# Inversion of the chunk matrices: levels 16 and 32 computed as two column halves, level 64 as one quadrant

## The reference, cut to what matters

```python
L = jnp.where(tri_strict, jnp.einsum('bhnid,bhnjd->bhnij', k_beta, kc) * decay, 0.0)
A = L + jnp.eye(C, dtype=f32)
rhs = jnp.concatenate([vc * bc[..., None], k_beta * jnp.exp(gc)[..., None]], axis=-1)
sol = lax.linalg.triangular_solve(A, rhs, left_side=True, lower=True, unit_diagonal=True)
```

## Time and profile before

| | value |
|---|---|
| median of 3 runs | 2764.27 us (2758.3 to 2764.56) |
| profiled execution | 2765.13 us, its span 2763.1 us |
| PE busy | 2565.5 us, 93% of the span |
| DVE, ACT, POOL busy | 1444.8, 1075.4, 918.6 us |
| L1429 MATMUL | x384 records, 53.0 us, mean 284 ns |
| L1447 and L1444 MATMUL | x256, 280 ns and x128, 226 ns |
| inversion, layer 1 | 491.0 to 581.5 us of the span |
| inversion, layer 2 | 1619.9 to about 1713 us |

### The profile page before, as it was taken

One profiled execution on the slowest core, in us unless ns is written; L12 is line 12 of the kernel. 1 busy time (PEld: TensorE's weight loads), 2 busy tenths in 40 slices (PEclk: granted clock), 3 DMA queues, 4 the chain that ended last, 5 costly groups with the idle time before them and its releaser, 6 DMA issues. The chain is left out here.

```text
span 2763.1 us, 32968 instructions
## 1 busy us (share of the span) xinstructions
PE 2565.5 (93%) x12929; PEld 2070.7 (75%) x12929; DVE 1444.8 (52%) x2609; ACT 1075.4 (39%) x1872; POOL 918.6 (33%) x402
## 2 busy tenths in 40 slices
PE   5989899899989999989988989999999997899998
PEld 3767768797867888757676878877788886786787
DVE  5289748654535541136993766454344206726323
ACT  3345464245332232243554523543333223236532
POOL 0532231112434444334222211134344443332343
PEclk8999999999999999999999989999999999999999
DMA  6211325643234432222132465422223324731232
GB/s 236 76 62 62 123 69 145 186 133 135 96 103 137 137 102 91 93 92 76 47 123 68 116 165 179 146 87 92 76 92 107 93 98 125 152 101 47 77 121 77
DMA packets 339836, 299.93 MB, mean 109 GB/s; under 512 B 56974, under 2 KB 319460, under 8 KB 338660
## 3 DMA queue, kind: packets, MB, share of 16 engines
q1 hardware_dynamic: 287716, 279.49, 32.5%
q10 hardware_dynamic: 51968, 18.35, 2.7%
HBM read 267.89 MB, written 29.93 MB: 108 GB/s over the span
## 5 line engine op out<-in xcount | busy, mean ns | idle before, releaser
L273 PE MATMUL ps<-hh,split 128*128 128x512 f32 x3808 | 1291.6, 407 | 39.4 <-POOL split L220 24.5
L220 POOL TENSOR_TENSOR split<-ring,split 128x1024 fp32r<-128x1024 f32 (+2 forms) x342 | 814.6, 2383 | 1428.4 <-ACT split L216 1428.4
L273 PEld LDWEIGHTS ps<-hh,split 128*128 128x128 f32 x3808 | 729.0, 191 | 212.5 <-POOL split L220 39.7
L273 PE MATMUL ps<-hl,split 128*128 128x512 f32 x1904 | 753.2, 396 | 0.0
L216 ACT ACTIVATE split<-ring 128x1024 fp32r<-128x1024 f32 (+2 forms) x342 | 347.6, 1018 | 893.1 <-PE ps L273 686.1
L273 PEld LDWEIGHTS ps<-hl,split 128*128 128x128 f32 x1904 | 365.4, 192 | 73.1 <-issue 8.4
L273 PE MATMUL ps<-split 128*128 128x512 f32 x1152 | 285.4, 405 | 9.0 <-DVE split L1095 7.1
L273 PEld LDWEIGHTS ps<-split 128*128 128x128 f32 x1152 | 218.6, 190 | 70.6 <-issue 14.7
L2169 PE MATMUL ps<-split 128*128 128x512 f32 x1056 | 240.2, 389 | 0.0
L2169 PEld LDWEIGHTS ps<-split 128*128 128x128 f32 x1056 | 198.1, 188 | 41.0
L560 POOL TENSOR_TENSOR split<-ring,split 128x1024 fp32r<-128x1024 f32 x32 | 76.1, 2378 | 338.2 <-ACT split L552 338.2
(11 more groups left out here) (408 smaller groups left out, 3178.2 us busy)
## 6 DMA issues: line engine op xcount, KB each, us to landing
ring<-in_w_in_dram SPq DMA_DIRECT2D x60, 1024.0 KB, 5.3
ring<-in_w_up_dram SPq DMA_DIRECT2D x44, 1024.0 KB, 5.1
ring<-in_w_ada_dram SPq DMA_DIRECT2D x64, 512.0 KB, 3.7
ring<-in_w_in_dram SPq DMA_DIRECT2D x34, 512.0 KB, 5.2
big<-in_w_ada_dram SPq DMA_DIRECT2D x16, 1024.0 KB, 8.5
ring<-in_w_down_dram SPq DMA_DIRECT2D x16, 896.0 KB, 4.6
ring<-in_w_swa_out_dram SPq DMA_DIRECT2D x8, 1024.0 KB, 5.0
ring<-in_w_dn_out_dram SPq DMA_DIRECT2D x8, 1024.0 KB, 5.0
```

The costliest lines, as they stand in the source:

```text
L220: on.tensor_tensor(halves(pt, nk)[1], slot(n, nk)[:, :, e * P:(e + 1) * P], halves(pt, nk)[0], ALU.subtract).then_inc(low_made, 1)
L273: ins = nc.tensor.matmul(ps[bank[gt]][0:m, :], w[:, k, :], r[:, k, :], start=(k == 0 and w is w_high and r is rhs[0]), stop=(k == nk - 1 a ...
```

## The change

It replaces the products of 128 rows by 128 stationary columns by smaller ones.

- Levels 16 and 32, first product: two matmuls for each head, one for each half of 64 columns (`HALVES`). Stationary are 64 columns of `lows`, moving are the 32 even-block columns of that half of `inv`; the results go to partitions 0 to 63 and 64 to 127 of the same 32 PSUM columns.
- Levels 16 and 32, second product: likewise two for each head, with 64 columns of `invt` stationary and 32 columns of `pc` moving.
- The masks of these levels have 32 columns in place of 64 and the DVE operation 128 columns in place of 256. The update of `inv` becomes two DVE operations of 64 partitions and 128 columns.
- Level 64: the first product takes the 64 rows and 64 columns that matter. A copy of 64 partitions replaces the mask. The second product contracts over 64 rows instead of 128. The mask `level64` goes; the table of constants is 128 columns narrower.

```diff
-    for s in LEVELS:
-        col = np.array([c for c in range(P) if (c // s) % 2 == 0])
-        parts[f"level{s}"] = ((np.arange(P)[:, None] // s) == (col[None, :] // s + 1))
+    for s in LEVELS[:-1]:
+        col = np.array([c for c in range(P // 2) if (c // s) % 2 == 0])
+        parts[f"level{s}"] = ((np.arange(P)[:, None] % (P // 2) // s) == (col[None, :] // s + 1))
...
+                    def pc(c, s):
+                        return wk[:, 8 + c % 2, 0:P if s < 64 else 2 * P].rearrange("p (h c) -> p h c", h=4)
+                    def product(e, rows, s):
+                        return ps[3 + e][rows, 0:P if s < 64 else 2 * P].rearrange("p (h c) -> p h c", h=4)
+                    HALVES = (slice(0, 64), slice(64, 128))
...
-                                        ins = nc.tensor.matmul(ps[3 + e][:, 64 * n:64 * n + 64], lows(g, c)[:, n, :],
-                                                               even_blocks(inv(g, c)[:, n, :], s), start=True, stop=True)
+                                        if s == LEVELS[-1]:
+                                            ins = nc.tensor.matmul(product(e, HALVES[1], s)[:, n, :],
+                                                                   lows(g, c)[0:64, n, 64:128], inv(g, c)[0:64, n, 0:64],
+                                                                   start=True, stop=True)
+                                            continue
+                                        for own in HALVES:
+                                            ins = nc.tensor.matmul(product(e, own, s)[:, n, :], lows(g, c)[:, n, own],
+                                                                   even_blocks(inv(g, c)[:, n, own], s), start=True, stop=True)
...
-                                            ins = nc.tensor.matmul(ps[5 + e][0:64, 64 * n:64 * n + 64], pc(c)[:, n, :],
-                                                                   invt(g, c)[:, n, 64:128], start=True, stop=True)
-                                        else:
-                                            ins = nc.tensor.matmul(ps[5 + e][:, 64 * n:64 * n + 64], invt(g, c)[:, n, :],
-                                                                   pc(c)[:, n, :], start=True, stop=True)
+                                            ins = nc.tensor.matmul(ps[5 + e][0:64, 64 * n:64 * n + 64], pc(c, s)[64:128, n, :],
+                                                                   invt(g, c)[64:128, n, 64:128], start=True, stop=True)
+                                            continue
+                                        for own in HALVES:
+                                            ins = nc.tensor.matmul(ps[5 + e][own, 32 * n:32 * n + 32], invt(g, c)[:, n, own],
+                                                                   pc(c, s)[:, n, :], start=True, stop=True)
...
-                                    nc.vector.tensor_tensor(pc(e), ps[3 + e][:, 0:256].rearrange("p (h c) -> p h c", h=4),
-                                                            over_heads(const(f"level{s}")), ALU.mult).then_inc(d_pc, 1)
+                                    if s == LEVELS[-1]:
+                                        nc.vector.tensor_copy(pc(e, s)[64:128], product(e, HALVES[1], s)).then_inc(d_pc, 1)
+                                    else:
+                                        nc.vector.tensor_tensor(pc(e, s), product(e, slice(0, P), s),
+                                                                over_heads(const(f"level{s}")), ALU.mult).then_inc(d_pc, 1)
...
-                                        ev = x[:, 2 * g + e, :].rearrange("p (b e s) -> p b e s", e=2, s=s)[:, :, 0, :]
-                                        nc.vector.tensor_tensor(ev, ev, ps[5 + e][:, 0:256].rearrange("p (b s) -> p b s", s=s),
-                                                                ALU.subtract).then_inc(d_t, 1)
+                                        for own in HALVES:
+                                            ev = heads(x[:, 2 * g + e, :])[own, :, own]
+                                            ev = ev.rearrange("p h (b e s) -> p h b e s", e=2, s=s)[:, :, :, 0, :]
+                                            t = ps[5 + e][own, 0:P].rearrange("p (h b s) -> p h b s", h=4, s=s)
+                                            ins = nc.vector.tensor_tensor(ev, ev, t, ALU.subtract)
+                                        ins.then_inc(d_t, 1)
```

More of the change, by code:

```diff
@@ L1291, in corner @@
                         return a[0:64, :, 64:128]
-                    def pc(c):
-                        return wk[:, 8 + c % 2, 0:2 * P].rearrange("p (h c) -> p h c", h=4)
+                    def pc(c, s):
[3 more added lines that the diff above has]
+                    HALVES = (slice(0, 64), slice(64, 128))
                     ADA_P3, ADA_P4 = 32, 32 + 6 * 12
```

## The result

The changed kernel took 2767.47 us, the median of 20 runs (2756.18 to 2771.04); the kernel before took 2760.91 us beside it (20 runs, 2750.04 to 2765.7). The ratio is 1.0021, 95% interval 1.0012 to 1.0031: slower by 0.2%, where I had forecast faster by 0.2%. The time lies inside my range (2750 to 2768 us), at its upper edge, by luck: what brought it there was not in the sum. The direction is wrong.

A forecast was written before the change was run, and what follows sets the result against it. The inversion was taken as bound by PE's own work, with DVE behind it. Gains of 3.5, 1.5 and 1.5 us less 0.9 made 5.6 us, so 2764.27 became 2758.7 us, range 2750 to 2768.

The forecast's parts named there:

- The first products: Levels 16 and 32: each first product takes 0.70 us with entry, saving 0.17 and 0.08 us a step.
- The second ones: Levels 16 and 32: the second products take 1.07 us instead of 1.73, with the two halves passing side by side.
- rival 3: Column halves don't run side by side, so steps take longer: +15 us, 2779 us; chance 0.05.
- Level 64 without POOL: Level-64 steps not held by POOL save 0.25 us each through smaller first products; six of eight gain 1.5 us together.
- The mask: DVE's masks at levels 16 and 32 get 0.14 us shorter, 0.28 instead of 0.42, but bring nothing since not waited for.
- What is late next: Levels 16 and 32: PE newly waits 0.18 and 0.17 us for DVE's updates, cutting a step's 0.71 us saving by 0.35.
- undisturbed step: Step of level 16 or 32 without a POOL operation: 0.35 us shorter; ten such steps gain 3.5 us.
- Steps with a POOL operation: Levels 16 and 32: POOL holds the update, so each step gets 0.15 us longer; six lose 0.9 us.
- the first steps: First step of each layer's inversion, at half clock: savings count double there, 1.5 us extra over both layers.
- the step of rows 9: Level-64 step where PE already waits 1.09 us for a mask that POOL holds: claimed to gain 0.
- a fall of the clock: Sign against the forecast: PE's clock falls in the inversion beyond the first step; no time was assigned to it.
- Rival 2: POOL and DMA hold DVE more often, and PE waits for it in the inversions: +5 us, 2770 us; chance 0.14.

The follow-up runs named there:

- e11: Changed kernel with POOL's subtraction in eight pieces and, at levels 16 and 32, one fill moved behind the second products: 2741.47 us, 0.9922 of the kernel before.
- e1: Changed kernel with POOL's subtraction cut to one of eight row blocks, the rest left out of the result: 2746.11 us, 0.9939 of the kernel before.
- e5: Kernel before with only the column halves of levels 16 and 32, level 64 as it was: 2763.87 us, 1.002 of the kernel before.
- e12: Kernel before with an extra DVE operation of 256 columns ahead of the mask of each layer's first level-64 step: 2765.13 us, 1.0002 of the kernel before.
- e17: Kernel before with an extra DVE operation of 512 columns ahead of the mask of each layer's first level-64 step: 2759.72 us, 0.9992 of the kernel before.
- e3: Changed kernel with six unused 512-column matmuls ahead of the second products of each layer's first level-64 step: 2758.63 us, 0.9992 of the kernel before.
- e10: Kernel before with only level 64 changed, plus six unused 512-column matmuls ahead of its first step's second products: 2758.33 us, 0.9977 of the kernel before.
- e16: Kernel before with only level 64 changed, plus two unused 512-column matmuls ahead of its first step's second products: 2759.99 us, 0.9997 of the kernel before.
- e8: Complete changed kernel with POOL's subtraction as eight operations of one row block each: 2748.44 us, 0.996 of the kernel before.
- e6: Kernel before with only level 64 changed, levels 16 and 32 as they were: 2770.48 us, 1.0037 of the kernel before.
- e14: Kernel before with only level 64 changed, plus two 512-column matmuls between its first step's two second products: 2776.96 us, 1.0051 of the kernel before.
- e4: Changed kernel with both first products back to back and PE's fills moved to where it waits: 2762.41 us, 0.999 of the kernel before.

## Why the prediction was wrong

**What held.** The first products cost 0.19 and 0.10 us less (forecast 0.17 and 0.08). The second ones took 1.05 us where nothing waits behind them (e11, 502.57 to the fill at 503.62; forecast 1.07): two halves pass side by side, and rival 3 is out. TensorE: Matmul & The Clock Gate of the Trainium skill says in Part 3 that a weight load overlaps matmuls in flight only where the row groups differ. 32 records in 1.05 us on all 128 rows don't fit that sentence, as the earlier trace rows didn't. Level 64 without POOL gained 0.22 to 0.30 us (6.21 and 6.30 to 5.99; forecast 0.25). The mask was 0.29, the new waits stood where the forecast put them.

**Step "What is late next": mis-sized.** I set the two waits at 0.18 and 0.17 us; the rows show 0.22 and 0.17. But the steps from start to start show 1.35 - 1.07 = 0.28, then 1.52 - 1.14 = 0.38 and 0.05 in the last piece (its other 0.08 is the way into the next half-array records): 0.71 us instead of 0.35. The idle time in a row counts from the modelled end of the last record. Where nothing waits the next record starts before that end (the transposes at 506.23, the end of the second products at 506.39), so a wait also costs this overlap. The pair of updates lasts 0.58, not 0.48. So an undisturbed step gained 0.16 to 0.19 us instead of 0.35, and those that took 7.26 us before nothing (7.24 in layer 2 of after, 7.25 to 7.27 in e1).

**Steps with a POOL operation: mis-sized.** Forecast 0.15 longer; 7.87 and 7.88 became 8.44, 0.57 longer. Six such steps make 6 x 0.42 = 2.5 us more than counted, as an estimate: four of the six show it, the other two are the steps of 9.86 and 8.78 us (8.70 and 8.71 in e5, without a fall, against 8.23 and 8.24 in e12 and e17, which have the old products). With the ten undisturbed steps short of some 0.19 each, 1.9 us, this uses up 4.4 of the 5.6 us. e3 (0.9992, about 2 us faster) and e5 (slower, without a fall) bracket what is left: near nothing. The 1.5 us of the first steps no run settles, since their half clock differs in length from one execution to the next (10.2 and 17.1 us before, 10.2 and 13.7 after); there is a slip in it too, 1.7 less 0.35 is 1.35 and not 1.2.

**The step that failed: "In the step of rows 9 POOL holds the mask itself and PE waits for it, so that step gains 0".** It gains nothing, and it isn't harmless. PE does less ahead of a fixed end and waits 1.48 us, and its clock falls for 10 and 17 us. In after that step and the next take 10.25 and 9.31 us in layer 1, before 7.77 and 7.26; in layer 2 they are 10.26 and 11.47, before 7.76 and 7.44. This is 11 us over both layers. e3 shows by filling the wait that the wait brings the fall, e10 and e16 show it for the quadrant alone, and e1 and e8 by taking away what makes PE wait. I had named a fall of the clock among what would make me wrong but priced it nowhere, although show what half clock costs.

**Rival 2** has the right place (POOL holds DVE, and what DVE does is now in PE's chain) and the right sign, by a mechanism that it didn't name: not more held steps, but the clock behind one.

**What stays open.** What exactly the clock follows. That the wait is needed at this place is shown; that the lighter products before it are needed as well is not. For it speaks: a wait of 1.48 us behind 64x64 products stood before every long fall (after, e6, e14, both layers, six of six), while 1.47 and 1.74 us behind full-size products gave none and 1.75 us one of 3.4 us. Waits of 1.03 us or less behind the light products gave none (e3, e10, e16). Against a simple rule speak the column halves: behind waits of 1.41 and 1.42 us there 3.4 us at half clock followed in three of six cases (layer 1 of after and both layers of e3, not layer 2 of after nor either layer of e5), and behind 1.42 to 1.62 us in e11 none in three; in e4 1.29 us brought 6.8 us and 1.76 us 3.4. One difference was not held fixed: in e12, e16 and layer 1 of e17 the half-clock stretch of the first step was 17.1 us long, in after, e6 and e14 10.2 to 13.7. In e3 and in layer 2 of e10 it was as short as there and no long fall followed, so it doesn't decide alone. Layer 2 of e17 (10.2 us, then 1.75 us behind full-size products, then 3.4 us) is the one case that compares with e6 in this. And the rest of e5's 0.2% is not located.

## What to carry to other kernels

When another engine's end is fixed, making PE's work before it smaller buys a wait, and the clock that falls behind the wait can cost more than the wait: here waits of 1.48 us were followed by 10 and 17 us at half clock, and the two steps at this place got 4.5 and 6.5 us longer. So ask of each step that PE waits in after the change, not only of those that get shorter: what stands before the wait, how long is it, and what did the granted clock do there in the trace. Look first for what holds the awaited engine (here one long POOL operation, which in pieces let DVE through), move independent matmuls into the wait, and see where the wait went (in e4 it only moved). With DVE let through the smaller products were worth 6 us, and with the moved fill 17.

## What the runs showed of the hardware that I had not expected

- Two DVE add steps with two SBUF operands each took 3.02 us beside POOL's subtraction of 1024 columns, and 0.99 without it; beside the same subtraction in eight pieces one took 0.53 to 0.74, though POOL's total rose from 2.36 to 4.34 us. The copy out of PSUM in the middle of the eight pieces took its usual 0.43.
- Six added matmuls made the kernel faster (e3 against after, e10 against e6: 8 and 17 us by the ratios).
- The idle time printed before a record understates what a wait costs: 0.22 and 0.17 us in the rows were 0.28 and 0.43 in the step (the second with the 0.05 of the last piece).
- The mean granted clock of a kernel's runs, 0.968 to 0.974 here, told more than the time of one profiled execution: the profiled e6 took 2762.05 us, its median was 2770.48.
